# Decode attention of one hybrid decoder step: queries x keys in four 32-partition quadrants, and a 32x32 block transpose on VectorE in place of TensorE

## What is computed

```python
def dilated_attention_sample(q, k, v, kv_buf):
    k_all = jnp.concatenate([kv_buf[:, :, 0].astype(jnp.float32), k], axis=1)
    v_all = jnp.concatenate([kv_buf[:, :, 1].astype(jnp.float32), v], axis=1)
    ...
    for _, d in ATT_PATTERNS:                      # (128,1), (512,4), (2048,16)
        idx = w_buf + jnp.arange(t)[:, None] - steps[None, :] * d
        ...
        s = jnp.einsum('bthd,btkhd->bthk', q, kg) * (HEAD_DIM ** -0.5)
        lse = jax.nn.logsumexp(s, axis=-1)
        p = jnp.exp(s - lse[..., None])
        outs.append(jnp.einsum('bthk,btkhd->bthd', p, vg))
    return combine_branches(outs, lses)
```

## Time and profile before

| | before |
|---|---|
| median of 3 runs | 1511.13 us (1510.36 to 1512.04) |
| span of the profiled execution | 1508.3 us |
| profiled execution's own time, beside its span | the span alone is shown; the median lies 2.8 us above it |
| PE busy | 1495.7 us, 99% |
| DVE busy | 823.5 us, 55% |
| ACT busy | 585.3 us, 39% |
| DMA | 296.59 MB, 197 GB/s mean |

### The profile page before, as it was taken

The page is one execution under the profiler, slowest core; times in us unless marked ns, Lnnn a source line. Parts: engine busy times, 40 slices in busy tenths (PEclk is TensorE's granted clock), DMA queues, the critical chain, the costliest instruction groups (busy, mean ns, idle before and its releaser), DMA issues.

```text
span 1508.3 us, 27166 instructions
## 1 busy us (share of the span) xinstructions
PE 1495.7 (99%) x11095; PEld 1414.8 (94%) x11095; DVE 823.5 (55%) x1074; ACT 585.3 (39%) x793; POOL 220.8 (15%) x316
## 2 busy tenths in 40 slices
PE   9999999999999999999999999999999999999997
PEld 8999777777778999999999999999999999999997
DVE  6669899964566677444444444444444433333433
ACT  6333434446545354333333333333333323333332
POOL 7864344500630000000000000000000000000100
PEclk9999999999999999999999999999999999999998
DMA  7547899999886444444444444444444444444442
GB/s 269 188 159 246 292 368 374 339 361 358 341 320 261 155 152 142 154 154 146 147 153 149 144 152 153 144 148 153 148 146 151 153 145 150 154 147 148 153 153 99
DMA packets 83283, 296.59 MB, mean 197 GB/s; under 512 B 9985, under 2 KB 11137, under 8 KB 82817
## 3 DMA queue, kind: packets, MB, share of 16 engines
q1 hardware_dynamic: 82624, 294.34, 56.1%
q10 hardware_dynamic: 576, 1.08, 0.2%
HBM read 289.31 MB, written 5.43 MB: 195 GB/s over the span
## 4 chain that ended last, share of the span: by engine, by line
PE 88%; issue 5%; DVE 4%; ACT 1%; POOL 1%; DMA 0%; SPq 0%; POOLq 0%; ACTq 0%
PE ps L1990 19%; PE ps L1988 19%; PE ps L1989 19%; PE ps L1834 7%; PE ps L1836 3%; PE ps L1872 3%; PE ps L1878 3%; PE ps L1873 3%; PE ps L1646 2%; PE ps L1675 2%; PE ps L1941 1%; PE ps L1939 1%; PE ps L1940 1%; DVE wlo L982 1%; PE ps L1620 1%
## 5 line engine op out<-in xcount | busy, mean ns | idle before, releaser
L1288 DVE TENSOR_TENSOR wlo<-raw,whi 128x1024 fp32r<-128x1024 f32 x264 | 325.1, 1231 | 520.0 <-ACT whi L859 519.9
L859 ACT ACTIVATE whi<-raw 128x1024 fp32r<-128x1024 f32 x264 | 279.9, 1060 | 606.2 <-PE ps L1990 601.7
L1988 PE MATMUL ps<-xh,whi 128*128 128x320 f32 x1400 | 432.6, 309 | 0.0
L1990 PE MATMUL ps<-xh,wlo 128*128 128x320 f32 x1400 | 432.6, 309 | 0.0
L1989 PE MATMUL ps<-xl,whi 128*128 128x320 f32 x1400 | 432.6, 309 | 0.0
L1990 PEld LDWEIGHTS ps<-xh,wlo 128*128 128x128 f32 x1400 | 262.8, 188 | 0.0
L1989 PEld LDWEIGHTS ps<-xl,whi 128*128 128x128 f32 x1400 | 262.8, 188 | 0.0
L1988 PEld LDWEIGHTS ps<-xh,whi 128*128 128x128 f32 x1400 | 262.8, 188 | 0.0
L1989 PE MATMUL ps<-hl,whi 128*128 128x320 f32 x696 | 215.1, 309 | 0.0
L1990 PE MATMUL ps<-hh,wlo 128*128 128x320 f32 x696 | 215.1, 309 | 0.0
L1988 PE MATMUL ps<-hh,whi 128*128 128x320 f32 x696 | 215.1, 309 | 0.0
(11 more groups left out here) (332 smaller groups left out, 1803.5 us busy)
## 6 DMA issues: line engine op xcount, KB each, us to landing
raw<-in_w_gu SPq DMA_DIRECT2D x176, 512.0 KB, 3.4
raw<-in_w_dn SPq DMA_DIRECT2D x88, 512.0 KB, 3.5
raw<-in_w_in SPq DMA_DIRECT2D x78, 512.0 KB, 5.1
kv<-in_ck SPq DMA_DIRECT2D x76, 512.0 KB, 6.3
kv<-in_cv SPq DMA_DIRECT2D x64, 512.0 KB, 7.2
raw<-in_w_out SPq DMA_DIRECT2D x32, 512.0 KB, 3.5
raw<-in_cv SPq DMA_DIRECT2D x16, 512.0 KB, 7.7
out_kv<-z SPq DMA_DIRECT2D x2, 1280.0 KB, 12.3
```

What stands on the lines that cost most here:

```text
L859: act.activation(whi[:, j % SPL, :], raw[:, j % RAW, :], ACT.Copy).then_inc(S["w_hi"], 1)
L1288: v.tensor_tensor(wlo[:, j % SPL, :], raw[:, j % RAW, :], whi[:, j % SPL, :].bitcast(F32), ALU.subtract) \
L1988: t_.matmul(out, whi[:, slot, w], ah[:, k, :], start=(k == 0), stop=False)
L1990: last = t_.matmul(out, wlo[:, slot, w], ah[:, k, :], start=False, stop=(k == 2 * units - 1))
```

## The change

The keys of a batch are dealt to the quadrants: each 32-partition quadrant of PE's output holds one quarter of the 1280 keys (KQ = 320), for four heads a step. So there are four K steps (KS = 4) in place of five, in relative slots 0 to 3, each with 16 more output columns a matmul in sum (64 matmuls of 64 columns x 3 or 2 pieces). The exponentiated tile is 128 x 4 x 352 (KW = 320 + 32 new keys), and a 32x32 block transpose of it, on DVE, is what `values` needs. START_OF is one slot later each, and the values begin at 6: so the values and the output stand in the same slots as before.

What each engine does differently, per batch:

- PE: the transposes L1665 and L1669 are gone. New: `sum_probabilities` ("norm"), four matmuls of one column in bank 6 that fold the partial sums of the four quadrants, in relative slot 5. The new keys' scores are eight matmuls of 32 columns in one quadrant. The new keys' values are four full matmuls (vn is now 128x1024, mostly zero).
- ACT: the copies L685 and L690 are gone. New: `spread_maxima` (4 copies of 32x4), `spread_bias` (4 copies of 32x4), and four exponentials of 128x352 with four accumulators in place of one of 128x1344.
- DVE: four masks of 128x320 in place of five of 128x256; the new keys' mask, reduce and maximum on 32 partitions; `maxima` (a reduce of 32x16) between the two ACT steps; `turn_probabilities` (the transpose of 128x1408, for batches 0 and 1 also 128x128), two memsets (`no_new`), and the reciprocal of the folded sums from PSUM (`inverse_sums`), in relative slot 5 after the low half.
- SP: a K step comes in two loads of 768 and 512 KB, in rows of 2 KB; the ring is kept by addresses (KV_FROM, KV_AFTER, KV_DONE).

The waits that stand in other places are in the core of the diff:

```diff
-START_OF = (36, 42, 48, 54, 60, 66, 72, 78)
-TURN, VALUES, OUTPUT = 5, 7, 12
+START_OF = (37, 43, 49, 55, 61, 67, 73, 79)
+TURN, VALUES, OUTPUT = 5, 6, 11
...
-            for b in batches(s, TURN + 1):
-                end.append((7, ("pt", b, 2)))
-            for step in range(KN):
+            for step in range(KS):
                 for b in batches(s, step):
                     end.append((6, ("score", b, step)))
+            for b in batches(s, TURN):
+                end.append((6, ("norm", b)))
             for b in batches(s, VALUES):
                 end.append((4, ("av", b)))
-            for b in batches(s, TURN):
-                end += [(6, ("pt", b, 0)), (7, ("pt", b, 1))]
...
-                    "pt": lambda: ("pt_moved", 4 * key[1] + (key[2] + 1 if key[2] < 2 else 4)),
-                    "score": lambda: ("s_masked", 6 * key[1] + (key[2] + 1 if key[2] < 4 else 6)),
+                    "score": lambda: ("s_masked", KS * key[1] + key[2] + 1) if key[2] < KS - 1 else ("new_masked", key[1] + 1),
+                    "norm": lambda: ("s_sum", key[1] + 1),
...
+            def spread_maxima(b):
+
+                act.wait_ge(S["s_max"], b + 1)
+                for j in range(4):
+                    act.activation(quads[0:32, j, :], smax[32 * j:32 * j + 32, 0:4], ACT.Copy).then_inc(S["s_spread"], 1)
+
+            def spread_bias(b):
+
+                act.wait_ge(S["s_top"], b + 1)
+                for j in range(4):
+                    act.activation(sbias[32 * j:32 * j + 32, 0:4], sbias[0:32, 4:8], ACT.Copy, scale=-SCALE).then_inc(S["s_bias"], 1)
+
             def exponent(b):
-                act.wait_ge(S["s_max"], b + 1)
-                act.activation(sall[:], sall[:], ACT.Exp, bias=smax[:, 7:8], scale=SCALE, accum_out=rsum[:, 0, b:b + 1]).then_inc(S["p_exp"], 1)
...
+                act.wait_ge(S["s_bias"], 4 * b + 4)
+                for g in range(4):
+                    act.activation(sall[:, g, :], sall[:, g, :], ACT.Exp, bias=sbias[:, g:g + 1], scale=SCALE,
+                                   accum_out=psums[:, b, g:g + 1]).then_inc(S["p_exp"], 1)
...
+            def turn_probabilities(b):
+
+                dve.wait_ge(S["p_exp"], 4 * b + 4)
+                if b:
+                    dve.wait_ge(S["v_used"], KEY_TILES * b)
+                if b < LATE:
+                    if b == 0:
+                        dve.wait_ge(S["x_rot"], PAIRED)
+                    step(v.transpose(ptk_late[b][:], sall[:, :, KQ:KW]), wait=False)
+                v.transpose(ptk[:].rearrange("p a n -> p (a n)"), sall[:].rearrange("p a n -> p (a n)")).then_inc(S["p_turned"], 1)
+                dve.wait_ge(S["p_turned"], b + 1)
+                if b < DEC_BATCH - 1:
+                    no_new((slice(32, 64), slice(64, P)) if b + 1 < 4 else (slice(0, 32), slice(64, P)))
+
+            def inverse_sums(b):
+                dve.wait_ge(S["p_sums"], b + 1)
+                v.reciprocal(rsum[:, b:b + 1], ps[:, 6, 0:1]).then_inc(S["s_sum"], 1)
...
+                for b in batches(s, 4):
+                    maxima(b)
                 for b in batches(s, TURN):
-                    dve.wait_ge(S["p_exp"], b + 1)
-                    v.reciprocal(rsum[:, 1, b:b + 1], rsum[:, 0, b:b + 1]).then_inc(S["s_sum"], 1)
+                    turn_probabilities(b)
+                    inverse_sums(b)
...
+            def sum_probabilities(b):
+
+                fill(6, "norm", b)
+                pe.wait_ge(S["fold_ready"], 1)
+                pe.wait_ge(S["p_exp"], 4 * b + 4)
+                for g in range(4):
+                    last = t_.matmul(ps[32 * g:32 * g + 32, 6, 0:1], fold[:], psums[:, b, g:g + 1], start=True, stop=True,
+                                     tile_position=(0, 32 * g))
+                last.then_inc(S["p_sums"], 1)
```

More of the change, by code:

```diff
@@ L453, in build @@
         for s in range(SLOTS):
[L454 to L455 removed]
+            here = [("k", b, 2 * i + part) for i in range(KS) for b in batches(s, i) for part in range(2)]
+            here += [("v", b, j) for b in range(DEC_BATCH) for j in range(KEY_TILES) if START_OF[b] + VALUES + j // 2 == s]
             KV_ORDER += here
@@ L458, in build, with kv_size @@
         KV_AT = {key: n for n, key in enumerate(KV_ORDER)}
+        def kv_size(kind, i):
+            return 512 * (K_PARTS[i % 2][1] - K_PARTS[i % 2][0]) if kind == "k" else ATT_WIDTH
+        KV_FROM, KV_AFTER, held, in_raw, pos = [], [], [], None, 0
+        for n, (kind, _, i) in enumerate(KV_ORDER):
+            size = kv_size(kind, i)
+            if kind == "v" and (in_raw is None or n - in_raw >= KV - 1):
+                KV_FROM.append(None)
+                KV_AFTER.append([] if in_raw is None else [in_raw])
+                in_raw = n
+                continue
+            if pos + size > KV_ROOM:
+                pos = 0
+            KV_AFTER.append([m for m, lo, hi in held if lo < pos + size and hi > pos])
+            held = [x for x in held if x[0] not in KV_AFTER[n]] + [(n, pos, pos + size)]
+            KV_FROM.append(pos)
+            pos += size
+        KV_DONE = []
+        for n in range(len(KV_ORDER)):
+            KV_DONE.append(max([KV_DONE[n - 1] if n else -1] + KV_AFTER[n]))
+        assert all(KV_DONE[n] >= n - KV for n in range(len(KV_ORDER)))
         TURNS = sorted(range(DEC_BATCH), key=lambda b: LATE_SLOTS[b] + 1.5 if b < LATE else START_OF[b] + OUTPUT)
@@ new lines, in mask_scores, with maxima, no_new @@
+                dve.wait_ge(S["s_masked"], KS * b + KS)
+                v.tensor_tensor(smax[own, 0:4], smax[own, 0:4], smax[own, 4:8], ALU.max).then_inc(S["s_max"], 1)
+            def maxima(b):
+                dve.wait_ge(S["s_spread"], 4 * b + 4)
+                v.tensor_reduce(sbias[0:32, 4:8], quads[0:32].rearrange("p j g -> p g j"), AX.X, ALU.max).then_inc(S["s_top"], 1)
+            def no_new(quadrants):
+                for q in quadrants:
+                    step(v.memset(sall[q, :, KQ:KW], NEG))
@@ L1163, in _ @@
                     evict(s, 3)
-                for step_ in range(KN):
+                for step_ in range(KS):
                     for b in batches(s, step_):
@@ new lines, in scores @@
+                for part, (c0, c1) in enumerate(K_PARTS):
+                    n = KV_AT["k", b, 2 * i + part]
+                    pe.wait_ge(KV_IN[n % KV], 16 * (n // KV + 1))
+                    keys = kv_place(n).rearrange("p (c h n) -> p c h n", h=2, n=256)
+                    for half in range(2):
+                        for j in range(4):
+                            last = t_.matmul(ps[32 * j:32 * j + 32, 6, 64 * c0:64 * c1], qst[:, b % 2, 2 * i + half, :],
+                                             keys[:, :, half, 64 * j:64 * j + 64], start=(half == 0), stop=(half == 1), tile_position=(0, 32 * j))
@@ L1778, in end @@
                         turn_output(b)
-                for b in batches(s, TURN + 1):
-                    turn_probabilities(b, 2)
-                for step in range(KN):
+                for step in range(KS):
                     for b in batches(s, step):
                         scores(b, step)
+                for b in batches(s, TURN):
+                    sum_probabilities(b)
                 for j in range(0, KEY_TILES, 2):
```

212 lines of the change are left out of this document (103 added, 109 removed).

## The result

The changed kernel takes 1874.6 us (1866.8 to 1877.5) against 1510.7 (1509.4 to 1512.0): 1.240 times as long, 95% interval 1.2386 to 1.2418. Forecast were 1532 us and a range of 1510 to 1548. The sign was right, the size wrong by a factor of 17 in what was added: 364 us in place of 21. The cause of nearly all of it stands in a line of the diff that the prediction never priced.

What follows compares the result with a forecast made beforehand. PE, busy 99% of the span, was taken as the bound. Waits of 12.2 + 18.4 = 30.6 us less 9.5 gave +21.1: span 1508.3 to 1529.4, plus 2.8 for the median, 1532 us; range 1510 to 1548.

Steps and rivals of the forecast that it cites:

- the part on SP's queue: SP's load queue: K loads change size, not bytes, and ask for the same releases; 0 to 1 us, taken as 0.
- Rival F: K loads: rows of 2 KB at a DMA share of 0.98 make the ring late; +10 us, 1542; chance 0.03.
- PE's net gain: PE's issued work: 12.2 and 1.8 us saved, 2.6 and 1.9 added; 9.5 us off PE, between 5 and 11.
- The sum of a batch: PE, four one-column matmuls per batch: 0.32 us each batch, 2.6 us for eight.
- the new keys' scores: PE, eight matmuls of 32 columns in one quadrant: 0.48 us a batch against 0.25 before, 1.9 us for eight.
- The three waits at the sum: PE at `sum_probabilities` in slots 42, 54 and 84, waiting for the exponentials: 3.7, 4.4 and 4.1 us, together 12.2.
- Four exponentials: ACT, ahead of the sum: 0.48 us for each exponential of 352 elements, 1.9 us for four against 1.42 before.
- the other five batches: At the sum: the chain has the project and value groups beside it and ends about when PE arrives; nothing charged.
- The chain behind the sum: Bank 6's next user waits for DVE's reciprocal behind transpose and memsets: 8 x (0.7 + 1.6) = 18.4 us, bounds 5.6 and 31.
- the 1.6 us of lateness: DVE's load grows 2.2 us per batch, so its lateness, up to 2.2, stays for most of it; 1.6 taken.
- Sum of waits: PE's waits before the sum, 12.2 us, and behind it, 18.4 us: 30.6 us.
- The clock, rival B: PE's clock falls to half in the long waits, on top of the main forecast: +6 us, 1538; chance 0.12.

Runs made afterwards that it cites:

- whole tiles: The changed kernel with keys dealt so that each V load is again 128 neighbouring rows, K read from SBUF with the same step: 1550.3 us, ratio 1.0256.
- no maximum, reciprocal first: Changed kernel with V tiles loaded whole, no maximum subtracted before the exponential, and DVE's reciprocal ahead of the block transpose: 1532.6 us, ratio 1.0141.
- the eight kernels of the table: The changed kernel with V tiles loaded whole, and seven versions of it with further edits to maxima, transpose, sum or reciprocal: 1532.6 to 1566.7 us.
- without the maxima: Changed kernel with V tiles loaded whole, no maximum subtracted before the exponential, the eight copies and DVE's reduce between them left out: 1538.8 us.

## Why the prediction was wrong

The step that failed is in the part on SP's queue: "the K loads change size, not bytes, and ask for the same releases; 0 to 1 us". It looked at the K loads, the release order and the number of bytes, and not at the access pattern of the V loads, which the diff changes in one line. It was put at 0; alone it costs the kernel before 349 us, and with whole tiles the changed kernel is rid of 324 of its 364. The trace of before had half of the warning: DMA share 0.98 at 200 to 250 us, so any load that uses fewer engines must show. That few groups mean few engines, it could not show. Rival F held the right resource with the wrong half of the diff (runs of 2 KB, which cost nothing) and a price of 10 us.

With the V loads whole, the remaining steps can be read one by one; the forecast was 1532 for what is now 1550.3.

- PE's net gain, forecast 9.5 (5 to 11). In the kernel with the least half clock (no maximum, reciprocal first), span 1530.1: 1508.3 + 25.0 of gaps + 5.1 for 10.2 us of half clock leave 8.3 us of gain. That is the most it can be, as half clock costs nothing while PE waits; with none of the 5.1 it is 3.2. A straight line through the eight kernels of the table (span less gaps, against half clock) gives 7.8, an estimate. So it is right as far as the runs tell. The sum of a batch takes 0.2 us on PE where I took 0.32, the new keys' scores 0.47 where I took 0.48.
- The three waits at the sum, forecast 3.7, 4.4 and 4.1: 4.8, 5.0 and 4.7. Mechanism and places right, each 0.6 to 1.1 too small, from two prices read too low. The groups of the kernel after:

```profile
L734 ACT ACTIVATE sall<-sall,sbias 128x352 f32<-128x352 f32 x32 | 18.4, 578 | 0.2
L729 ACT ACTIVATE sbias<-sbias 32x4 f32<-32x4 f32 x32 | 6.5, 204 | 6.2 <-DVE sbias L1077 5.6
L723 ACT ACTIVATE quads<-smax 32x4 f32<-32x4 f32 x32 | 6.4, 199 | 0.6
L1093 DVE STREAM_TRANSPOSE ptk<-sall 128x1408 f32<-128x1408 f32 x8 | 13.0, 1629 | 0.0
```

  Four exponentials take 2.3 us, not 1.9: each takes 578 ns, where my line through a copy of 256 elements and the exponential of 1344 gave 480. Why isn't shown; each has an accumulator read of 0.19 us beside it. Four copies take 0.87 (172.21), where L706's, of other size, took 0.57.
- In the other five batches nothing was charged at the sum; 4.9 us stood there. For 3.0 of them (batches 1 and 3) PE waits not for the exponentials but for bank 6: ACT reads the projection out of it (L812) only behind the four exponentials, the last of which ends at 302.96 in batch 3, with PE's sum at 304.0.

```profile
303.25 0.68 ACT L812 ACTIVATE xs<-ps 128x640 f32<-128x640 f32 x1
```

- The chain behind the sum, forecast 18.4: 8.9 us, keys and projection together, of which 5.9 follow a sum. The transpose was right (1.6 forecast, 1.63 measured; the short one of 128 elements takes 304 ns, which makes 1.04 ns an element and 0.17 us fixed). What failed is the 1.6 us of lateness added to each batch. In the three batches in which PE has waited 5 us at the sum, DVE has caught up: batches 0 and 2 wait less than 0.3 and 1.2 us behind it here, and 1.9 and 4.6 without the maxima. The two terms were added as if independent, and aren't. Why the other five batches too waited less than forecast (2.0 us at most) no run shows.
- Waits that had no term: 5.8 us at the values and 5.6 elsewhere.
- Sum of waits: forecast 30.6, measured 39.8.
- The clock, rival B, priced at 6 with a chance of 0.12: 27.3 us at 0.50, up to 13.7 us of work. It should have been part of the main case: such a stretch begins in or right after each of the three waits of 4.7 us or more, and at four of those between 1.8 and 2.1 us. The waits of 2.1 us at 304 us and of 2.7 us at 379 us have none.

In spans, the repaired kernel missed the forecast by 19.7 us (1549.1 against 1529.4). Of these 9.2 are waits. The other 10.5 are the clock and what the gain was short of 9.5; with a gain of 8.3 the clock has cost 9.3.

## What to carry to other kernels

Read each DMA's access pattern in a diff as closely as its bytes: what counted here is how many entries the slowest dimension has (4, 8 and 16 were slow, 64 and 128 not), and perhaps whether the load covers all partitions. A change of data layout that spares an engine a transposition can be paid for in the load. Where an engine without slack gets a handshake with another (maxima to one quadrant and back), lateness moves from one waiting instruction to the next, and what helped here was to shorten the chain. And a kernel whose PE never idled has a full clock to lose: here 40 us of waits brought 27 us of half clock, some 9 us more (an estimate from the line above).

## What the hardware showed unexpectedly

Loads of 512 KB in packets of 4 KB, the same but for the number of row groups, moved some 100 GB/s at 4 groups, 240 at 16 (at a full busy share) and 400 at 64 or whole. Four loads of 32 partitions each cost the changed kernel 85 us over whole tiles, where 16 groups cost the kernel before 106. A DMA share of 1.0 is thus no sign that a load runs at full rate; bytes per second are.
